# The gates' scratch in DRAM turned from a token-tile-major to a key-major layout

## The reference, cut to what matters

```
def peer_ffn(h, w_pq, sub_keys, u_emb, v_emb):
    ...                                  # 8 heads, top 16 of 128 x 128 product keys
    expert = i1 * PEER_KEYS + i2         # one of 16384 experts, 128 picks per token
    gate = jax.nn.softmax(best_v, axis=-1)
    def block(args):
        h_blk, e_blk, g_blk = args
        u = u_emb[e_blk]
        a = jnp.einsum('bthkd,btd->bthk', u, h_blk)
        act = (jax.nn.gelu(a) * g_blk)
        return jnp.einsum('bthk,bthkd->btd', act, v_emb[e_blk])
```

## Time and profile before

| | |
|---|---|
| median of 3 runs | 4029.95 us (4027.95 to 4037.29) |
| span of the profiled execution, first to last instruction | 4016.0 us |
| TensorE, VectorE, ScalarE, GpSimd busy | 92%, 76%, 36%, 41% of the span |
| mean granted clock of TensorE | 0.965 of full speed |
| DMA, whole span | 848.44 MB in 314926 packets, 211 GB/s |
| spread part, 2700 to 3045 us | TensorE busy 292.70 us of 345.00 |
| value part, 3100 to 3900 us | TensorE busy 795.47 us, VectorE 791.60 us of 800.00; 387 GB/s |

### The profile page before, as it was taken

The page is one execution under the profiler, slowest core; times in us unless marked ns, Lnnn a source line. Parts: engine busy times, 40 slices in busy tenths (PEclk is TensorE's granted clock), DMA queues, the critical chain, the costliest instruction groups (busy, mean ns, idle before and its releaser), DMA issues. The chain is left out here.

```text
span 4016.0 us, 61930 instructions
## 1 busy us (share of the span) xinstructions
PE 3708.7 (92%) x21687; PEld 3273.7 (82%) x21687; DVE 3049.5 (76%) x5229; ACT 1460.9 (36%) x2548; POOL 1648.8 (41%) x1269
## 2 busy tenths in 40 slices
PE   6999999998899999898998999988896999999996
PEld 5766677666577886688898998988886999999996
DVE  5677776777753604369999998777764999999998
ACT  3455555566552424322222222224341222222222
POOL 2433434343322121015565555462213555656562
PEclk9999999999999999899999999999998999999998
DMA  2111111111353312148888888884659999999995
GB/s 86 48 48 54 53 37 53 44 53 49 112 186 125 122 53 80 73 134 294 315 333 325 297 317 291 317 309 156 243 192 342 391 388 390 389 387 390 387 392 200
DMA packets 314926, 848.44 MB, mean 211 GB/s; under 512 B 28624, under 2 KB 122064, under 8 KB 310736
## 3 DMA queue, kind: packets, MB, share of 16 engines
q1 hardware_dynamic: 201232, 400.92, 28.7%
q0 software_dynamic: 110592, 402.70, 26.4%
q10 hardware_dynamic: 2880, 41.94, 2.6%
HBM read 726.96 MB, written 118.49 MB: 211 GB/s over the span
## 5 line engine op out<-in xcount | busy, mean ns | idle before, releaser
L1918 POOL DMA_INDIRECT join_urow<-in_u_rows,select_row_now x384 | 519.7, 1353 | 509.6 <-DVE join_rows L2219 226.1
L2668 POOL DMA_INDIRECT spread_vrow<-in_v_rows,spread_row_of x384 | 536.3, 1397 | 391.3 <-DVE spread_y L2738 279.7
L163 PE MATMUL spread_banks<-spread_ahi,spread_vhi 128*128 128x384 f32 (+1 forms) x2048 | 637.3, 311 | 35.5 <-DVE spread_acc L2728 14.7
L163 PE MATMUL select_products<-h_hi,shared_pair_hi 128*128 128x256 f32 (+2 forms) x1856 | 609.4, 328 | 62.9 <-DVE shared_raw_low L1736 49.8
L164 PE MATMUL spread_banks<-spread_alo,spread_vhi 128*128 128x384 f32 (+1 forms) x2048 | 635.0, 310 | 1.8 <-issue 1.8
L165 PE MATMUL spread_banks<-spread_ahi,spread_vlo 128*128 128x384 f32 (+1 forms) x2048 | 635.4, 310 | 1.3 <-issue 1.3
L165 PE MATMUL select_products<-h_hi,shared_raw_low 128*128 128x256 f32 (+2 forms) x1856 | 604.9, 326 | 3.2 <-issue 3.1
L164 PE MATMUL select_products<-h_lo,shared_pair_hi 128*128 128x256 f32 (+2 forms) x1856 | 605.5, 326 | 2.2 <-issue 2.0
L163 PE MATMUL shared_carry<-shared_wide_hi,shared_w_hi 128*128 128x512 f32 x1408 | 557.9, 396 | 28.5 <-DVE shared_wide_lo L591 11.2
L164 PE MATMUL shared_carry<-shared_wide_lo,shared_w_hi 128*128 128x512 f32 x1408 | 553.8, 393 | 0.0
L165 PE MATMUL shared_carry<-shared_wide_hi,shared_w_lo 128*128 128x512 f32 x1408 | 553.2, 393 | 0.0
(11 more groups left out here) (305 smaller groups left out, 6685.3 us busy)
## 6 DMA issues: line engine op xcount, KB each, us to landing
spread_vraw<-in_peer_v SPq DMA_DIRECT2D x128, 512.0 KB
shared_raw<-in_select_pairs SPq DMA_DIRECT2D x112, 512.0 KB
gates<-spread_stage ACTq DMA_DIRECT2D x20, 2048.0 KB, 16.6
spread_act<-gelu_u SPq DMA_DIRECT2D x128, 320.0 KB
spread_graw<-gates SPq DMA_DIRECT2D x128, 320.0 KB
gelu_u<-front SPq DMA_DIRECT2D x100, 320.0 KB, 2.5
shared_w_raw<-in_w_mix SPq DMA_DIRECT2D x56, 512.0 KB, 3.5
shared_w_raw<-in_w_cross SPq DMA_DIRECT2D x32, 512.0 KB, 3.5
```

Source lines behind the costliest of these rows:

```text
L163: nc.tensor.matmul(out, whi, xhi, start=(first and i == 0), stop=False)
L1918: nc.gpsimd.indirect_dma_start(picks.slots[s][:], None, u_rows, bass.IndirectOffsetOnAxis(row_now[:, t, j:j + 1], 0)).then_inc(row_loaded[ ...
L2668: nc.gpsimd.indirect_dma_start(v_slots[s][:], None, v_rows, bass.IndirectOffsetOnAxis(row_of[:, par, t, j:j + 1], 0)).then_inc(row_loaded[ ...
```

## The change

The scratch gets the shape [KEYS, P, ND, P]: key, row, token tile, token, without the eight unused keys. In this layout all that `load_gates` reads for one key is contiguous, 2560 bytes for each row (partition) and 320 KB in all; before, it read five runs of 512 bytes per partition. The store of a token tile writes, for each partition, one run of 512 bytes per key, at a distance of 327680 bytes; before, one store (a quarter of the keys) wrote one run of 16384 bytes per partition. Number, size, order, queues and waits of the DMA instructions stay the same, and so does every other instruction.

```
             def load_gates(e, i):
-                sync.dma_start(graw[:, e].rearrange("p (n t) -> p n t", t=P),
-                               g_out.rearrange("n p a t -> a p n t")[i].rearrange("a p n t -> (a p) n t")).then_inc(g_loaded[e], 16)
+                sync.dma_start(graw[:, e], g_out[i].rearrange("a p n t -> (a p) (n t)")).then_inc(g_loaded[e], 16)
...
                         part = slice(i * KEYS // NS, (i + 1) * KEYS // NS)
-                        nc.scalar.dma_start(g_out[tt, :, part, :], stage[:, part, :]).then_inc(stored, 16)
+                        nc.scalar.dma_start(g_out.rearrange("k p n t -> n p k t")[tt, :, part, :], stage[:, part, :]).then_inc(stored, 16)
...
-    gelu_u, gates = scratch("gelu_u", [KEYS, P, TD]), scratch("gates", [ND, P, KEYS + 8, P])
+    gelu_u, gates = scratch("gelu_u", [KEYS, P, TD]), scratch("gates", [KEYS, P, ND, P])
```

## The result

The changed kernel takes 4071.15 us (4066.44 to 4072.15, 4 runs) against 4031.05 (4027.95 to 4037.29) of the kernel before: +40 us by the medians, whose quotient is 1.0100; the ratio estimated from all the runs is 1.0085 with a 95% interval of 1.0068 to 1.0102. On another chip, later, it was 4075.70 against 4019.15, +57 us, ratio 1.0142 (1.0120 to 1.0164). The prediction had the sign and the place right, and +98 us.

What follows compares the result with a forecast made beforehand. VectorE and TensorE bound the value part, TensorE the spread steps, a late u tile the gaps. +83 +4 +16.4 -5 = +98 us on 4016.0, 4114; with 13.95 to the median, 4128 us (0.50, 4105 to 4150; 8-in-10 range 4060 to 4190).

Steps and rivals of the forecast that it cites:

- The issue holds ScalarE: Spread part, each store burst: ScalarE, issuing 1024 packets per engine, stands until all but 110 have gone, 30.2 us plus about 3.
- the second form of the first rival: Store issue holds ScalarE only until the fourth store is taken in: +14.2 us four times, 4092 us; whole rival 0.24.
- U: Moment ScalarE is free again after issuing a token tile's stores; forecast 2797 us, from an issue start at 2763.8.
- What queues behind U: GELU, splits and first halves waiting on ScalarE after the store issue: eviction starts 15.4 us later, 20.8 us later than before.
- The packet: Price of a 512-byte store packet on a DMA engine: 33 ns, so 33.8 us of DMA time per burst.
- The eight steps behind it are TensorE's and stay: Spread part, eight steps of a token tile after each gap: bound by TensorE, 31.26 us busy of 32.00, no change.
- The last burst: Behind the fifth store: ScalarE is free 33.2 us after 2998.12, first gate load at 3047.0 against 3030.65, +16.4 us.
- The u tiles landing early and gaining nothing: Gap behind each store: u tiles no longer alternate with 653 ns packets and land early, no gain because ScalarE stands.
- The loads: Gate tile loads in longer runs: 4.5 us for one tile beside gathered rows, 0.5 for the first tiles, -5 us.
- No hold: Rival, 0.24: the store issue doesn't hold ScalarE, `stored` decides; +10.4 us four times, last gate load +5.5, 4072 us.
- Line rate: Rival, 0.07: 512-byte writes cost no more per byte than long ones, below 24 ns a packet; faster, about 4004 us.
- Dearer writes: Rival, 0.15: 512-byte store packets cost 50 to 66 ns, each burst adds 17 to 34 us, 4215 us and up.

## Why the prediction was wrong in size

**The issue holds ScalarE: right, and mis-sized.** The term of the sum that failed is "ScalarE stands until all but 110 have gone", 33.2 us. It measured 21.3. The open packets I read from SyncE were those of transfers already taken in, not a cap on what may be open. In 2762 to 2777.2, the end of the third issue, q10 had moved 7091 of the 12288 packets issued:

```profile
q10 hardware_dynamic: 7091, 3.62, 84.1%
```

325 per engine were open, three times what I thought possible: 256 of the transfer just taken in and 69 ahead of it (94 and 82 at the second and the fourth issue by the same count). A transfer is taken in whole, once the ones ahead are down to 70 to 95 here, and to between 75 and 104 in the kernel with 16 issues. So the fourth went in with 256 + 82 packets to go. I had this reading as the second form of the first rival (4092 us, U at 2790.4); the measured U was 2784.2. One issue (22 us faster) and sixteen (24 us slower) showed it. What queues behind U was read rightly: 16.7 us for 15.4. The difference is the clock, for which 1 us a gap was added without a row: the granted clock was 0.69 in 2784 to 2790, and the matmuls of the first half took 0.21 us for 0.12.

**The packet: a little dear.** 29.4 ns for 33. With one issue the store lands at 36.1 us for 37.7, although q1 takes more of it than the 3.9 us that I carried over: 19.2% of 2761 to 2797, 6.9 us.

**"The eight steps behind it are TensorE's and stay": wrong.** They became 3.1 us longer each, +12.4. I took the busiest engine of the earlier trace rows, 31.26 of 32.00, and passed over VectorE's 30.17 beside it. VectorE needs some 4.8 us for the operands of a step and lives from three or four steps of lead, made during the store. Held back, ScalarE held up step 0, and VectorE idled 31.8 us in one piece in the gap (13.8 before):

```profile
2802.20 1.22 DVE L2696 TENSOR_TENSOR front<-spread_iota,front 128x2048 f16<-128x2048 f16 x1 [31.77 <-PE spread_banks L2851]
```

The four gaps together: forecast 4 x 20.8 + 4 = +87, measured +43.2 for the evictions and +12.4 for the steps. So one step of the prediction was too large by 44 us and another, put at nothing, was worth 12; the second hid a part of the first.

**The last burst: +16.4 forecast, +6.1 measured,** by the same hold of 21.4 us for 33.2.

**The u tiles landing early and gaining nothing: right.** 90.1 us of waits became 15.3 and the gap still grew. With one issue, where nothing holds ScalarE, they are 13.8: they land 7.1 us after their issue. Packet by packet is not the whole of it beside short packets. The u tile issued at 2763.6 in that kernel moved nothing before 2768, and then q10 moved three packets for two of q1:

```profile
q10 hardware_dynamic: 1996, 1.02, 98.0%
...
q1 hardware_dynamic: 179, 0.56, 74.3%
q10 hardware_dynamic: 272, 0.14, 28.1%
```

The first line is 2764 to 2768, 125 packets per engine; the others are 2768 to 2770.

**The loads: -5 forecast, -21 and -6 in the runs.** "VectorE and TensorE are full, so I count nothing" read one execution as all of them. Its 8.4 us of VectorE idle time was not the most that could be gained: other executions of the kernel before have 9 us more. A DMA share of 1.05 may have been the sign of it. The entry, where I put the whole gain, gave half of the 5 us: VectorE's first split of the second group's `vraw` starts 55.8 us after the first gate load, for 57.7 before,

```profile
3088.32 1.23 DVE L2651 TENSOR_TENSOR spread_vlo<-spread_vraw,spread_vhi 128x1024 fp32r<-128x1024 f32 x1 [13.43 <-ACT spread_vhi L2914]
...
3147.21 1.23 DVE L2650 TENSOR_TENSOR spread_vlo<-spread_vraw,spread_vhi 128x1024 fp32r<-128x1024 f32 x1 [16.32 <-ACT spread_vhi L2913]
```

(before, then after) and over all traces 54.5 to 56.2 with long loads at the entry, 57.5 to 58.8 with short ones. The rest of the 10 us by the traces lies in the loop, for which I counted nothing.

**The rivals.** No hold: its first form said 4072 us, and 4071 was measured, but by luck. The issues took 21.34 us, not under 2, and the kernel in which nothing is held is 22 us faster; its +42 for the gaps was the measured +43.2 of another cause, and the 13.95 us, most of which were not there, stood in for the steps' +12.4. Line rate: q10 at 29.4 ns per 512 bytes moves 279 GB/s on 16 engines; it would have needed under 24 ns. The Trainium skill ("DMA: Bandwidth & Descriptors", Specifications) lets 512 bytes suffice for line rate; this trace disagrees, as the earlier trace rows already did. Dearer writes: a 512-byte write costs no more than a 512-byte read (29.4 ns for 32.0), and the 327680 bytes between runs cost nothing visible; for this rival 4128 + 5 x 17 is 4213, not 4215, and nothing hangs on it.

What stays open: why the loads give 21 us on one chip and 6 on another, what moves the part ahead of the first store by up to 13 us, and what sets the 1.2 us of an issue in a row of sixteen.

## What to carry to other kernels

A layout in DRAM has two ends: cut short the runs on the side whose transfer nobody waits for, and count what a long list of packets does to the engine that issues it, which may have other work behind it; one long transfer here was free to issue where four held the engine 21 us. When two engines stand within a few per cent in a stretch, look at which of them lives from a lead: here the change took that lead, and VectorE became the bound. And where DMAs run at their full share, one trace is one draw: take the spread of the runs before calling a wait small.

## What the runs showed of the hardware

- Packet time on an engine is a fixed part and a part by bytes. Stores: 29.4 ns for 512 bytes, 49 for 1024, 165 for 4096, 653 for 16384; loads: 32.0 for 512, 173 for 4096. An estimate from the stores: 10 ns and 0.039 ns per byte.
- Queues share an engine. Beside packets of 16384 bytes a 512 KB load took 17.30 us, beside 4096 bytes 5.3, beside 512 bytes 7.0, and alone 3.8. Long packets alternate one for one (174 of 16384 bytes and 172 of q1 in 2770.6 to 2778 of the kernel before); beside 512-byte packets the load first waited 4 us, some 125 packets per engine, and then passed at 1.5 packets of the store for one of its queue (2.7 in 2769.4 to 2771.4 of the changed kernel, 374 and 138). The Trainium skill ("DMA: Bandwidth & Descriptors", Queues, rings and completion order) has an engine go round the queues and take 9 to 17 descriptors from one before it switches. These runs agree with the going round, not with the 9 to 17: by these counts it is one to three of the profile's packets.
- An issuing engine is held in two ways: until the packets ahead of it are down to 70 to 100 per engine (5.2 to 8.7 us an issue here), and by some 1.2 us an issue in a row of short transfers (16 issues, 18.91 us, 29 packets open). A single transfer of 1024 packets per engine took 0.43 us to issue.
